# Modulation's weight chunks asked for by GpSimd instead of SyncE, and the gate maxima's rows spread by a store and a load instead of matmuls

## The chip, the core and the metric

One core of one Trainium2 chip runs the whole kernel. The metric is the device time in microseconds of one execution. All engines (TensorE or PE, VectorE or DVE, ScalarE or ACT, GpSimd or POOL, and SyncE or SP, which only issues transfers) work side by side and wait for each other through semaphores. SP, ACT and POOL can each ask for DMA transfers. The transfers that SP and ACT ask for run as "hardware_dynamic" queues in the profile, those of POOL as the "software_dynamic" queue. All share the same 16 DMA engines.

## The reference, cut to what matters

Two networks follow each other on 256 tokens of width 1024, in float32. Two places of them are touched.

```
# first_block: a conditioning vector makes six rows of 1024 per layer and stream
m  = (silu(c)     @ w_mod[i] + b_mod[i]).reshape(bsz, 6, d)     # w_mod: (2, 1024, 6144)
mc = (silu(c_ctx) @ w_mod[i] + b_mod[i]).reshape(6, d)
h_lat   = x * (1.0 + s1) + sh1
mix_lat = chunk_mlp(h_lat, ...)        # gelu(h @ a_w_in), norm, spatial mixing, @ a_w_out
x = layer_norm(DN_ALPHA * x + g1 * mix_lat, ...)
ffn_lat = peer_ffn(x * (1.0 + s2) + sh2, ...)   # queries, top 16 of 16384 experts for each of 8 heads
...
# second_block, mlstm: the running maximum m_t of the gates goes into every score's exponent
m_t     = jnp.maximum(log_inter, jnp.max(log_intra, axis=-1))
d_intra = jnp.exp(log_intra - m_t[..., None])
```

## The kernel before, in words

The first block starts with two works side by side. **Modulation** (`condition`) streams `w_mod` as 48 chunks of 1 MB (128 partitions x 2048 numbers) through a ring of 6 landing places. PE multiplies each chunk with the conditioning columns, and the sums become the rows `m`. Eight chunks make one quarter row set (`q`). The rows are stored to DRAM (`modulation`) and read back where the mixer needs them spread over all partitions. **The mixer** (`first_mix`) streams its own weights as 64 chunks of 256 KB through a ring of 4. ACT rounds a chunk to its high part (`weights_high`), DVE makes the low part (`weights_low`), and PE multiplies with both. Five split chunks can stand ready.

What each engine does next is written out by hand. Each work is a generator that yields slot numbers, `Aside.up_to` runs a work up to a slot, and `run` goes through the slots. So each engine has one fixed order, in which modulation and mixer are interleaved: a modulation chunk about every 3.5 slots, a mixer chunk every 2. SP issues both kinds of load in that order. It stops at the first load whose landing place is not free, and all later loads wait behind it. The stores of `m` and the loads of whole rows (`g_row`, `v_rows`, `n_rows`, `x`, `ws`) stand in the same order.

After the mixer's last queries, DVE picks the first experts (`place`), and POOL begins the gathers: 768 transfers of 1 MB (128 rows of 8 KB each), in a ring of 8, which reuse the memory of the modulation chunks. `wait_rows_free` therefore holds the first gather back until all modulation chunks are used and stored. DVE, ACT and PE work off the gathered rows, and the rest of the first block is placed beside that.

The second block has 404 weight chunks of 512 KB and two layers. In each layer four mLSTM heads need the row of running maxima `rows[0:H, 3, P:]` (4 partitions x 256) on all 128 partitions. PE does this for each head `a` with one matmul against `pick_row`, right behind the head's scores. DVE subtracts it from the mask `past` out of PSUM (`logs`), ACT takes the exponential (`probs_set`), and DVE multiplies it with the scores (`weight`).

Of the kernel before, what the change touches and what calls it, by code (L numbers as in the profile page):

```python
# [25 lines left out]
P = 128  # L26
# [127 lines left out]
def condition(k, sem, buf):  # L154
# [20 lines left out]

    def bias(act):
# [72 lines left out]

    made.pool, made.bias, made.sync, made.stores, made.scalar, made.tensor, made.vector = (  # L250
# [5 lines left out]
def first_mix(k, sem, x, h, buf, given_landed, conditioned):  # L256
# [2052 lines left out]
N_COLS, COLS_HELD = 194, 256  # L2309
# [29 lines left out]
def second_block(k, x, out, ahead):  # L2339
# [5 lines left out]
    with ExitStack() as ctx:  # L2345
        def sem(name):
# [21 lines left out]
        v_ones_set, head_scores, logs_set, probs_set, head_weighed, head_sums, den_set, y_set = [  # L2368
            sem(n) for n in ("v_ones_set", "head_scores", "logs_set", "probs_set", "head_weighed", "head_sums", "den_set", "y_set")]
# [9 lines left out]
        def share(*plans):  # L2379
# [6 lines left out]
            warm=[P, P], bias_rows=[P, BIAS_ROWS, NC], wide_row=[P, D], decay=[P, H, 3 * P], cos=[P, SEQ], sin=[P, SEQ],  # L2386
            wgs_high=(gates_in, F32R), wgs_low=(gates_in, F32R),
            r_weight=[P, 2, 3 * P], inverse_diag=[P, 2, P], inverse_row=[P, SEQ],
            stats=[P, 8, 2, 6], moments=[P, 8, 2], spread=[P, 8], root=[P, 8], inverse=[P, 8],
            x_stats=[P, 2, 2, 6], x_moments=[P, 2, 2], x_spread=[P, 2], x_root=[P, 2], x_inverse=[P, 2],  # L2390
            gate_cols=[P, 16], den=[P, H, 2], den_inverse=[P, H, 2])
# [8 lines left out]
        ((_, weights_low, hT_high, hT_low, warm, bias_rows, wide_row, decay, cos, sin, wgs_high, wgs_low,  # L2400
          r_weight, inverse_diag, inverse_row, stats, moments, spread, root, inverse, x_stats, x_moments, x_spread, x_root,
          x_inverse, gate_cols, den, den_inverse), (_, yrT_low), (_, a1, a2, logs, weight), (_, pw, relu), (_, rg), _) = share(
# [3 lines left out]
        pick_row, past = hold(pick_row=[P, H, P], past=[P, SEQ])  # L2406
# [1426 lines left out]
```

## Time and profile before

| | |
|---|---|
| median of 3 runs | 3600.67 us (3595.59 to 3602.92) |
| the profiled execution, its own time | 3596.3 us |
| its span in the trace | 3594.2 us |
| PE busy | 3219.3 us (90%) |
| DVE busy | 2563.8 us (71%) |
| ACT busy | 1787.8 us (50%) |
| POOL busy | 875.9 us (24%) |
| DMA moved | 1157.76 MB, mean 322 GB/s |

The profiled execution took 2.1 us more than its span, and it lies 4.4 us under the median of the runs. An engine's busy share is a mean over stages that have different limits, so the stretches of the windows view matter more than the table. In that view each row is a stretch of the span with the busy time (and count of instructions) of each engine, then the granted TensorE clock as a share of full speed, the mean busy share of the 16 DMA engines, and the GB/s that they moved.

### The profile page before, as it was taken

To read this page: it belongs to the slowest core of one execution; us is meant where nothing else is said; L and a number is where in the kernel's file an instruction comes from. 1 tells how busy PE (TensorE), PEld (TensorE's weight loads), DVE (VectorE), ACT (ScalarE), POOL (GpSimd) and SP (SyncE) were. 2 spreads that over 40 slices of the span, in tenths; PEclk is the share of its full clock that TensorE was granted. 3 is DMA by queue.
4 is the path that set the end of the run, shared out by engine and by line. 5 is a ranking of instruction groups with operands and counts; after the bars stand their busy time and mean duration, and the time that the engine had idled before them with its cause. 6 is when DMAs were issued, how large, how long until landed. Compare 5 with 4: busy or idle time off the path is not lost. (4 is left out here: it accounts for less than half of the span.)

```text
span 3594.2 us, 38113 instructions
## 1 busy us (share of the span) xinstructions
PE 3219.3 (90%) x12760; PEld 2024.0 (56%) x12760; DVE 2563.8 (71%) x5158; ACT 1787.8 (50%) x3870; POOL 875.9 (24%) x778
## 2 busy tenths in 40 slices
PE   6879898898899989887888777889999999999998
PEld 3444444443354434446433222279878989988897
DVE  2577778878887787756877777578666758766675
ACT  2334554544564565544454444355564645555554
POOL 0024444444443444410444444400000000000000
PEclk8999999999999999999899999999999999999999
DMA  9979999999999999972999999966655656565564
GB/s 407 376 284 424 425 425 414 425 426 414 425 407 425 425 415 427 426 310 94 399 423 427 427 427 427 427 215 183 190 174 183 187 184 187 173 190 185 176 188 140
DMA packets 279755, 1157.76 MB, mean 322 GB/s; under 512 B 31059, under 2 KB 33619, under 8 KB 175110
## 3 DMA queue, kind: packets, MB, share of 16 engines
q0 software_dynamic: 110592, 805.36, 53.4%
q1 hardware_dynamic: 168582, 349.73, 29.2%
q8 instruction: 101, 1.65, 0.2%
q14 instruction: 96, 0.79, 0.1%
q10 hardware_dynamic: 384, 0.23, 0.0%
HBM read 1154.07 MB, written 1.15 MB: 321 GB/s over the span
## 5 line engine op out<-in xcount | busy, mean ns | idle before, releaser
L87 PE MATMUL psum<-rows,diag 128*128 128x512 f32 x3072 | 1473.5, 616 | 275.7 <-ACT diag L2246 273.7
L2202 DVE CUSTOM_DVE_ANT_0 rows<-rows,h 128x1024 f32<-128x1024 f32 x768 | 938.2, 1223 | 454.2 <-DMA rows<-in_p_uv,place 450.9
L2098 POOL DMA_INDIRECT rows<-in_p_uv,place x768 | 872.0, 1135 | 1353.1 <-PE psum L87 1053.5
L87 PEld LDWEIGHTS psum<-rows,diag 128*128 128x128 f32 x3072 | 558.5, 193 | 1091.8 <-ACT diag L2246 591.4
L3019 DVE TENSOR_TENSOR weights_low<-landing,weights_high 128x1024 fp32r<-128x1024 f32 x404 | 490.5, 1221 | 285.3 <-ACT weights_high L2966 282.2
L2966 ACT CAST weights_high<-landing 128x1024 fp32r<-128x1024 f32 x402 | 418.6, 1049 | 471.4 <-PE psum L87 328.6
L2233 ACT ACTIVATE acted<-dots 128x1 f32<-128x1 f32 x768 | 155.1, 202 | 835.3 <-DVE dots L2202 833.4
L87 PE MATMUL psum<-weights_high,hT_high 128*128 128x512 f32 x832 | 352.1, 423 | 14.7 <-DVE h L695 6.5
L2246 ACT ACTIVATE diag<-ident,weight 128x128 f32<-128x128 f32 x768 | 308.5, 402 | 70.4 <-ACT weight L2239 0.4
L87 PE MATMUL psum<-weights_high,hT_low 128*128 128x512 f32 x832 | 325.5, 391 | 0.0
L87 PE MATMUL psum<-weights_low,hT_high 128*128 128x512 f32 x832 | 325.4, 391 | 0.0
L2509 PE MATMUL psum<-hT_high,weights_high 128*128 128x256 f32 x1024 | 291.2, 284 | 1.6 <-DVE hT_low L2996 1.4
L2511 PE MATMUL psum<-hT_high,weights_low 128*128 128x256 f32 x1024 | 289.9, 283 | 0.0
L2510 PE MATMUL psum<-hT_low,weights_high 128*128 128x256 f32 x1024 | 289.9, 283 | 0.0
L2239 ACT ACTIVATE weight<-acted,share 128x1 f32<-128x1 f32 x768 | 226.2, 295 | 27.9
L87 PEld LDWEIGHTS psum<-weights_high,hT_high 128*128 128x128 f32 x832 | 156.8, 189 | 85.5 <-issue 26.8
L2509 PEld LDWEIGHTS psum<-hT_high,weights_high 128*128 128x128 f32 x1024 | 196.8, 192 | 3.4 <-issue 1.7
L2510 PEld LDWEIGHTS psum<-hT_low,weights_high 128*128 128x128 f32 x1024 | 196.8, 192 | 0.1
L2511 PEld LDWEIGHTS psum<-hT_high,weights_low 128*128 128x128 f32 x1024 | 196.6, 192 | 0.0
L87 PEld LDWEIGHTS psum<-weights_low,hT_high 128*128 128x128 f32 x832 | 157.1, 189 | 39.6 <-issue 11.0
L87 PEld LDWEIGHTS psum<-weights_high,hT_low 128*128 128x128 f32 x832 | 156.6, 188 | 34.1
L539 ACT CAST weights_high<-landing 128x512 fp32r<-128x512 f32 x128 | 78.3, 612 | 126.5 <-DMA landing<-in_a_w_in 69.1
(464 smaller groups left out, 3952.0 us busy)
## 6 DMA issues: line engine op xcount, KB each, us to landing
landing<-in_w_in SPq DMA_DIRECT2D x192, 512.0 KB, 3.8
landing<-in_w_ff SPq DMA_DIRECT2D x128, 512.0 KB, 4.0
landing<-in_w_mod SPq DMA_DIRECT2D x48, 1024.0 KB, 8.7
landing<-in_a_w_in SPq DMA_DIRECT2D x64, 256.0 KB
landing<-in_w_br SPq DMA_DIRECT2D x32, 512.0 KB, 3.5
rows<-in_p_uv,place POOLq DMA_INDIRECT x768
lat_landing<-in_b_w_in SPq DMA_DIRECT2D x48, 256.0 KB
landing<-in_a_w_out SPq DMA_DIRECT2D x32, 256.0 KB
```

What stands on the lines that cost most here:

```text
L87: return k.nc.tensor.matmul(out, lhsT, rhs, start=first, stop=last)
L539: S.copy(weights.high[:, n % SPLITS], landing[:, n % LANDING]).then_inc(chunk_high, 1)
L2098: k.nc.gpsimd.indirect_dma_start(rows[:, n % ROW_RING, :], None, k.given["p_uv"], bass.IndirectOffsetOnAxis(place[:, g % 4, c:c + 1], 0))\
L2202: V.tensor_tensor_reduce(u, u, token, 1.0, 0.0, ALU.mult, ALU.add, dots[:, g % 4, c:c + 1]).then_inc(dots_done, 1)
L2233: S.activation(acted[:, slot, c:c + 1], dots[:, slot, c:c + 1], ACT.Gelu_apprx_tanh).then_inc(gelu_done, 1)
L2239: S.activation(weight[:, slot, c:c + 1], acted[:, slot, c:c + 1], ACT.Copy, scale=share[:, slot, c:c + 1])\
L2246: S.activation(diag[:, n % DIAG_RING, :], k.ident[:, :], ACT.Copy, scale=weight[:, slot, c:c + 1])\
L2509: nc.tensor.matmul(to, mine.high, tokens.high, start=first, stop=False, skip_group_check=True)
L2510: nc.tensor.matmul(to, mine.high, tokens.low, start=False, stop=False, skip_group_check=True)
L2511: mm = nc.tensor.matmul(to, mine.low, tokens.high, start=False, stop=last, skip_group_check=True)
L2966: S.copy(weights.high[:, n % SPLITS], landing[:, n % LANDING]).then_inc(chunk_high, 1)
L3019: V.tensor_tensor(weights.low[:, n % SPLITS], landing[:, n % LANDING], weights.high[:, n % SPLITS].bitcast(F32), ALU.subtract).then_inc(ch ...
```

## The change

1. **Modulation's loads move from SP to POOL.** The 48 transfers stand in a new function `loads`, which POOL runs after its two memsets and before its index table and gathers. Each waits only for its own landing place. SP keeps the mixer's loads, the rows and the stores.
2. **Two new waits on SP.** The load of `x` waits until 3 modulation chunks are used, and the mixer's first load until 7 are used.
3. **The maxima's rows are spread by transfers.** ACT stores the four rows (4 KB) to a new DRAM tensor `gate_rows`, waits for the store two slots later, and loads them back to all 128 partitions (512 KB) as `m_rows`. The eight `pick_row` matmuls (4 heads x 2 layers) and the `pick_row` constant are gone. DVE reads `m_rows` in place of PSUM, and does so before it waits for the head's scores.
4. Buffers are laid out anew: `m_rows` is new, `past` moves, `warm` shrinks to one column, and `COLS_HELD` is 208, not 256.

```
+    def loads(pool):
+        for n in range(CHUNKS):
+            q, b = n // DB, n % DB
+            if n >= RING:
+                pool.wait_ge(chunk_used, n + 1 - RING)
+            pool.dma_start(landing[:, n % RING, :],
+                           given["w_mod"][q // 3][b * P:(b + 1) * P, q % 3 * WIDTH:(q % 3 + 1) * WIDTH])\
+                .then_inc(chunk_landed[n % RING], 16)
...
         sp.dma_start(cond[:, :, :], given["cond_cols"]).then_inc(cond_landed, 16)
-        for n in range(CHUNKS):
-            q, b = n // DB, n % DB
-            yield SLOTS[0] if n < RING else SLOTS[n - RING] + 0.5
-            if n >= RING:
-                sp.wait_ge(chunk_used, n + 1 - RING)
-            sp.dma_start(landing[:, n % RING, :],
-                         given["w_mod"][q // 3][b * P:(b + 1) * P, q % 3 * WIDTH:(q % 3 + 1) * WIDTH])\
-              .then_inc(chunk_landed[n % RING], 16)
...
+            if n == 0:
+                conditioned.wait_chunks(sp, 7)
             if n >= LANDING:
...
             conditioned.pool(pool)
             mixed1.pool(pool)
+            conditioned.loads(pool)
             chosen1.pool(pool, lambda engine: None, wait_rows_free)
...
             yield AHEAD + 1
+            conditioned.wait_chunks(sp, 3)
             sp.dma_start(x[:, 0:2, :], given["x"].rearrange("o (t p) d -> p (o t) d", p=P)).then_inc(tokens_landed[0], 16)
...
                 act.wait_ge(m_set, layer + 1)
+                act.dma_start(k.gate_rows[layer], rows[0:H, 3, P:]).then_inc(m_row_stored, 16)
                 S.activation(spare[0:H, :], li[0:H, :], ACT.Exp, scale=-1.0).then_inc(least_set, 1)
+                yield base + 22
+                act.wait_ge(m_row_stored, 16 * (layer + 1))
+                if layer > 0:
+                    act.wait_ge(logs_set, layer * H)
+                act.dma_start(m_rows[:, :, :].rearrange("p a t -> p (a t)"),
+                              k.gate_rows[layer].rearrange("a t -> (a t)").partition_broadcast(P)).then_inc(m_row_landed, 16)
...
-                        causal_scores(bank, qk, a)
-                        matmul(k, k.psum[:, bank + 1, 0:SEQ], pick_row[0:H, a, :], rows[0:H, 3, P:], True, True)\
-                            .then_inc(head_scores, 1)
+                        causal_scores(bank, qk, a).then_inc(head_scores, 1)
...
-                        dve.wait_ge(head_scores, layer * H + a + 1)
-                        V.scalar_tensor_tensor(mine[:, 0:SEQ], k.psum[:, bank + 1, 0:SEQ], -1.0, past[:, :], ALU.mult, ALU.add)
+                        if a == 0:
+                            dve.wait_ge(m_row_landed, 16 * (layer + 1))
+                            dve.wait_ge(more_landed, 64)
+                        if a >= 2:
+                            dve.wait_ge(probs_set, layer * H + a - 1)
+                        V.scalar_tensor_tensor(mine[:, 0:SEQ], m_rows[:, a, 0:SEQ], -1.0, past[:, :], ALU.mult, ALU.add)
...
                         yield base + 2
+                        dve.wait_ge(head_scores, layer * H + a + 1)
```

SP's queue at the very start of the program, before the change. `mod_used` counts modulation chunks that PE has used, `mix_low` mixer chunks that DVE has split:

```order
L186 DMA cond<-in_cond_cols 128x16
L193 DMA landing<-in_w_mod 128x2048 x6
L193 DMA landing<-in_w_mod 128x2048 [waits mod_used]
L3643 DMA x<-in_x 128x2x1024
L193 DMA landing<-in_w_mod 128x2048 [waits mod_used] x4
L321 DMA landing<-in_a_w_in 128x512
L193 DMA landing<-in_w_mod 128x2048 [waits mod_used] x2
L321 DMA landing<-in_a_w_in 128x512
```

The same place on SP, and behind it what POOL now issues:

```order
L196 DMA cond<-in_cond_cols 128x16
L3669 DMA x<-in_x 128x2x1024 [waits mod_used]
L329 DMA landing<-in_a_w_in 128x512 [waits mod_used]
L329 DMA landing<-in_a_w_in 128x512 x3
L204 DMA modulation<-m 2x512 [waits mod_taken]
```

```order
L174 MEMSET m 128x3072
L313 MEMSET keys 128x256
L182 DMA landing<-in_w_mod 128x2048 x6
L182 DMA landing<-in_w_mod 128x2048 [waits mod_used] x42
L2095 ISA
```

All modulation loads are gone from SP's order, and the mixer's first four loads stand together.

PE's queue at the first mLSTM head of the second block, before (`qk` are the head's scores):

```order
L87 MATMUL psum<-qk 128x256 x2
L87 MATMUL psum<-qk 128x128 x2
L87 MATMUL psum<-rows,pick_row 128x256
L87 MATMUL psum<-weights_high,hT_high 128x512
L87 MATMUL psum<-weights_low,hT_high 128x512
```

and now:

```order
L87 MATMUL psum<-weights_low,hT_high 128x512
L87 MATMUL psum<-weights_high,hT_low 128x512
L87 MATMUL psum<-qk 128x256 x2
L87 MATMUL psum<-qk 128x128 x2
L87 MATMUL psum<-weights_high,hT_high 128x512
```

The `pick_row` matmul is gone and the next weight chunk's products follow the scores at once.

ACT's queue where the maxima of a layer are ready, before (the CAST rows round weight chunks, the `spare` row is an exponential of the gates):

```order
L2966 CAST weights_high<-landing 128x1024
L2769 ACT_TABLE_LOAD
L2769 ACTIVATE spare<-li 4x256
L2930 ACTIVATE raw<-raw,cols 128x256 x4
L2966 CAST weights_high<-landing 128x1024 x5
```

and now:

```order
L2981 CAST weights_high<-landing 128x1024
L2775 DMA gate_rows<-rows 4x256
L2776 ACT_TABLE_LOAD
L2776 ACTIVATE spare<-li 4x256
L2945 ACTIVATE raw<-raw,cols 128x256 x4
L2981 CAST weights_high<-landing 128x1024 x2
L2783 DMA m_rows<-gate_rows 128x1024
L2981 CAST weights_high<-landing 128x1024 x3
```

The store stands ahead of the table load, and the load of `m_rows` stands two casts later.

## Rows read from the trace of the kernel before

**Rows 1.** The page, part 1: busy time, share and instructions of PE.
```profile
PE 3219.3 (90%) x12760; PEld 2024.0 (56%) x12760; DVE 2563.8 (71%) x5158; ACT 1787.8 (50%) x3870; POOL 875.9 (24%) x778
```

**Rows 2.** Windows view, stages of the whole span.
```profile
0.00:215.00 215.00, 170.73 (x956) 96.43 (x956) 102.81 (x183) 58.74 (x97) 3.55 (x8) 0.90 0.88 345
...
250.00:1550.00 1300.00, 1159.79 (x3196) 563.75 (x3194) 1010.98 (x2412) 690.02 (x1880) 577.29 (x494) 0.98 1.01 422
1550.00:1700.00 150.00, 124.89 (x480) 86.53 (x480) 91.56 (x150) 71.42 (x132) 7.22 (x10) 0.95 0.49 178
...
2380.00:3594.00 1214.00, 1200.34 (x6800) 1046.38 (x6798) 844.56 (x1163) 650.91 (x854) 0.00 (x0) 1.00 0.58 180
```

**Rows 3.** Windows view, stretches of the first stage.
```profile
50.00:95.00 45.00, 44.53 (x231) 24.88 (x228) 15.90 (x27) 14.78 (x24) 0.00 (x0) 1.00 1.02 419
95.00:110.00 15.00, 13.96 (x71) 6.96 (x71) 10.02 (x14) 7.99 (x13) 0.00 (x0) 1.00 0.97 368
110.00:135.00 25.00, 18.27 (x105) 12.38 (x106) 11.14 (x27) 6.60 (x12) 0.00 (x0) 0.86 1.02 419
135.00:165.00 30.00, 30.00 (x160) 17.29 (x159) 15.80 (x22) 8.56 (x13) 0.00 (x0) 1.00 0.98 371
...
175.00:215.00 40.00, 37.34 (x262) 27.73 (x260) 28.99 (x65) 12.68 (x22) 0.30 (x1) 0.90 0.37 124
```

**Rows 4.** Waits view, 50 to 166 us: total, times, longest.
```profile
ACT weights_high L539 <- DMA landing<-in_a_w_in: 36.9, 15, 4.9
...
ACT weights_high L539 <- DMA landing<-in_a_w_out: 20.7, 7, 5.3
```

**Rows 5.** Waits view of SP's queue, 1 to 215 us.
```profile
SPq L193 <- PE psum L87: 49.2, 20, 8.7
SPq L356 <- DMA modulation<-m: 4.7, 1, 4.7
```

**Rows 6.** Timeline from 0 us: start, duration, engine, what.
```profile
0.74 2.66 POOL L174 MEMSET m<- 128x3072 f32 x1 [0.29 <-POOLq L3827]
...
1.19 12.29 SPq L193 DMA_DIRECT2D landing<-in_w_mod  x7
3.34 0.31 POOL L307 MEMSET keys<- 128x256 f32 x1
```

**Rows 7.** Timeline of POOL: the first gather.
```profile
214.69 1.27 POOL L2098 DMA_INDIRECT rows<-in_p_uv,place  x1 [210.88 <-DVE place L2170]
```

**Rows 8.** Windows view, one microsecond behind it.
```profile
216.00:217.00 1.00, 0.76 (x7) 0.55 (x5) 0.00 (x0) 0.21 (x1) 0.73 (x1) 1.00 0.64 98
```

**Rows 9.** Line 330, two 512 KB rows asked for by SP beside the gathers.
```profile
L330 SPq DMA_DIRECT2D u<-modulation x2: 343/550/758, 221.9 to 222.2; - x2
...
DMA to landing us min/median/max: 8.7/10.4/12.0
```

**Rows 10.** Line 193, modulation loads issued between 30 and 100 us.
```profile
DMA to landing us min/median/max: 6.0/8.5/14.0
```

**Rows 11.** Timeline of ACT, the longest wait for a mixer chunk.
```profile
126.39 0.62 ACT L539 CAST weights_high<-landing 128x512 fp32r<-128x512 f32 x1 [5.32 <-DMA landing<-in_a_w_out]
```

**Rows 12.** All pick_row matmuls (each is recorded as two).
```profile
L87 PE MATMUL psum<-rows,pick_row x16: 374/426/478, 2456.7 to 3128.9; 4*128 4x256 f32 x16
```

**Rows 13.** Timeline of PE: one of the eight, and the next instruction.
```profile
2456.74 0.69 PE L87 MATMUL psum<-rows,pick_row 4*128 4x256 f32 x2
2457.36 0.50 PE L87 MATMUL psum<-weights_high,hT_high 128*128 128x512 f32 x1
```

**Rows 14.** Waits view of PE, 2378 us to the end: the longest entry.
```profile
PE psum L87 <- DVE hT_low L2994: 2.2, 2, 1.1
```

**Rows 15.** Timeline of ACT behind the maxima of layer 0.
```profile
2424.69 0.42 ACT L2769 ACTIVATE spare<-li 4x256 f32<-4x256 f32 x1
...
2430.55 1.05 ACT L2966 CAST weights_high<-landing 128x1024 fp32r<-128x1024 f32 x1 [1.00 <-PE psum L87]
```

**Rows 16.** DMA issues: KB each and us from issue to landing.
```profile
out_x<-x SPq DMA_DIRECT2D x4, 256.0 KB, 2.3
```

More of the change, by code:

```diff
@@ L248, in wait_used, with wait_chunks @@
         engine.wait_ge(chunk_used, CHUNKS)
+    def wait_chunks(engine, n):
+        engine.wait_ge(chunk_used, n)
+    made.loads, made.wait_chunks = loads, wait_chunks
     made.pool, made.bias, made.sync, made.stores, made.scalar, made.tensor, made.vector = (
@@ L2308 @@
 COL = {"norm1": 0, "norm2": 8, "norm3": 16, "m": 24, "r": 32, "b_qk": 48, "taps": 64, "tap_bias": 128, "b_r": 144, "b_ff1": 160, "b_gates": 192}
-N_COLS, COLS_HELD = 194, 256
+N_COLS, COLS_HELD = 194, 208
 IN_AT = 4 * D + 2 * HEADS
@@ L2367, in second_block @@
         convolved, conv_acted, roped, gated = [sem(n) for n in ("convolved", "conv_acted", "roped", "gated")]
-        v_ones_set, head_scores, logs_set, probs_set, head_weighed, head_sums, den_set, y_set = [
-            sem(n) for n in ("v_ones_set", "head_scores", "logs_set", "probs_set", "head_weighed", "head_sums", "den_set", "y_set")]
+        v_ones_set, m_row_stored, m_row_landed, head_scores, logs_set, probs_set, head_weighed, head_sums, den_set, y_set = [
+            sem(n) for n in ("v_ones_set", "m_row_stored", "m_row_landed", "head_scores", "logs_set", "probs_set", "head_weighed", "head_sums", "den_set", "y_set")]
         r_scores, r_weighed, r_sums, r_set = [sem(n) for n in ("r_scores", "r_weighed", "r_sums", "r_set")]
@@ L2399, in second_block @@
         weights_high = ahead.weights_high
-        ((_, weights_low, hT_high, hT_low, warm, bias_rows, wide_row, decay, cos, sin, wgs_high, wgs_low,
-          r_weight, inverse_diag, inverse_row, stats, moments, spread, root, inverse, x_stats, x_moments, x_spread, x_root,
-          x_inverse, gate_cols, den, den_inverse), (_, yrT_low), (_, a1, a2, logs, weight), (_, pw, relu), (_, rg), _) = share(
+        ((_, weights_low, hT_high, hT_low, bias_rows, wide_row, decay, cos, sin, wgs_high, wgs_low,
+          r_weight, inverse_diag, inverse_row, past, stats, moments, spread, root, inverse, x_stats, x_moments, x_spread, x_root,
+          x_inverse, gate_cols, den, den_inverse, warm), (_, yrT_low), (_, a1, a2, logs, weight), (_, pw, relu), (_, rg), _) = share(
             first, *shared, dict(lead=[P, LEAD]))
@@ L2405, in second_block @@
         hold(landing=[P, LANDING, PAIR, NC], cols=[P, DEPTH, COLS_HELD], wg=[P, DEPTH, DB, 2 * H])
-        pick_row, past = hold(pick_row=[P, H, P], past=[P, SEQ])
+        m_rows = hold(m_rows=[P, H, SEQ])
         with split_buffers(k, "f", [P, D_FF // P, SEQ]) as f:
@@ L2456, in _ @@
                 if n == LANDING:
-                    for dst, src in ((pick_row[0:H, :, :], given["pick_row"]), (past[:, :], given["past"]),
+                    for dst, src in ((past[:, :], given["past"]),
                                      (cos[:, :], given["rope_cos"]), (sin[:, :], given["rope_sin"]),
@@ L2571, in pe_heads @@
                         pe.wait_ge(gate_cols_set, layer + 1)
-                        pe.wait_ge(more_landed, 80)
+                        pe.wait_ge(more_landed, 64)
                     if a >= 1:
@@ L3278, in dve_rope @@
                     yield base
-                    dve.wait_ge(more_landed, 80)
+                    dve.wait_ge(more_landed, 64)
                     dve.wait_ge(raw_set, layer * 8 + 4 + i + 1)
@@ L3747, in program @@
         k.modulation = nc.dram_tensor("modulation", (2, DEPTH * 6 * D), F32).ap()
+        k.gate_rows = nc.dram_tensor("gate_rows", (DEPTH, HEADS, SEQ), F32).ap()
         with buffers(k, ident=[P, P], ones=[P, P], gap=[P, 96], x=[P, 4, D]) as (k.ident, k.ones, _, x):
@@ L3777, in constants @@
         "past": np.concatenate([np.where(r[None, :] >= r[:, None], 0.0, MASKED), np.zeros((P, P))], axis=1).astype(f),
-        "pick_row": np.repeat(np.eye(HEADS, dtype=f)[:, :, None], P, axis=2),
         "gla_prefix": (same & (r[:, None] <= r[None, :])).astype(f) / f(GLA_TAU),
```

8 lines of the change are left out of this document (4 added, 4 removed).

## The prediction

> **What bounds the kernel now.** I read the page first. PE is busy for 90% of the span [rows 1], but a mean hides that the stages have different limits, so I cut the span into stages with the windows view [rows 2]. From 250 to 1550 us the DMA engines are at share 1.01 and 422 GB/s: these are the gathers, a fixed number of bytes, and a stage like this only shifts as its start shifts. Between 1550 and 1700 us it is other work that has to end (share 0.49). From 2380 us on PE is busy for 1200.34 of 1214 us, while DMA moves 180 GB/s: here PE's instruction count sets the time. PE's longest entry in the waits of that block is 2.2 us in total [rows 14]. So an instruction taken from PE there is gained in full, and nothing else counts there unless it makes PE wait.
>
> The first stage, to 215 us [rows 2], ends with the first gather, which waits for DVE's picks (`place`) and not for the modulation chunks [rows 7]. What comes before the picks splits in two [rows 3]. From 50 to 165 us two things are near their limit together. DMA moves 419 GB/s in 50 to 95 us with PE busy for 44.53 of 45 us. In 135 to 165 us PE is busy for all 30 us and DMA falls to 371 GB/s. From 175 to 215 us DMA is at share 0.37 and PE at 37.34 of 40 us: queries, scores and picks, which no load holds up. So the end of the stage is the time at which the mixer's loads and products are done, plus a tail that the change leaves alone.
>
> **Part one, modulation's loads on POOL.** Who waits for a load in this stage? ACT waits 36.9 + 20.7 = 57.6 us for mixer chunks between 50 and 166 us, in 22 waits [rows 4]. SP itself stands 49.2 us at modulation loads whose landing place is not free, in 20 waits [rows 5], and the mixer's loads queue behind these. That speaks for the change. But ACT's waiting is not all on the path. With DMA at share 1.02 the bytes are what takes long, and the change moves the same bytes. I therefore cost the stage by what it adds to or takes from bytes before the tail.
>
> *A later start, +3.0 us.* SP's first modulation load is issued at 1.19 us. POOL is free for its first at 3.34 + 0.31 = 3.65 us [rows 6], which is 2.5 us later. The trace has no plain load from POOL. The nearest row is the first gather: issued at 214.69, and in 216 to 217 us the first 98 GB/s [rows 7, 8]. At 422 GB/s that is 0.23 us of moving, so about 2.1 us pass from request to first bytes. SP has a latency too. The lag lies between 2.5 (equal latencies) and 4.6 us (none on SP). I take 3.0, since a latency of near the same size on SP is likely. From 50 to 165 us the DMA engines are hardly ever out of work [rows 3], so all of it counts.
>
> *More unneeded bytes, +2 us.* Before, a modulation chunk lands 8.5 us (median) after its request, since all loads share one queue [rows 10]. The other direction can be read beside the gathers: two rows of 512 KB asked for together land 8.7 us and 12.0 us after their requests at 221.9 and 222.2 us [rows 9]. The second took 3.6 us alone, so 0.524 MB / 3.6 us = 146 GB/s, a third of the total, while 1 MB gathers got the rest. Half a megabyte against one: it looks as if one transfer of each queue is served in turn. A 256 KB mixer chunk against 1 MB modulation chunks would then get a fifth, 85 GB/s, or 3.1 us a chunk, as long as modulation has requests open. Modulation's ring of 6 would fill first and stay fuller. From nothing to all of the ring's missing part, which I estimate from 8.5 us at 2.5 us a chunk (1.049 MB / 422 GB/s) as 8.5 / 2.5 - 1 = 2.4 chunks, this brings forward 0 to 2.4 chunks or 0 to 6 us. I take 2, because once the ring is full modulation asks only as fast as PE uses.
>
> The Trainium skill, DMA: Bandwidth & Descriptors, section Queues, rings and completion order, says that each DMA engine round-robins between the queues it has work for, a packet at a time. The third above agrees with it in this trace.
>
> *Smoother DMA, -2.0 us.* In 95 to 110 us DMA moved 368 GB/s instead of the 422 of the gathers, which is (1 - 368/422) x 15 = 1.9 us of lost moving with PE not full (13.96 of 15). POOL would fill this hole. The dip of 135 to 165 us, (1 - 371/422) x 30 = 3.6 us, lies beside a full PE and gives nothing.
>
> *The stall, -2.0 us.* Between 110 and 135 us PE is idle for 25 - 18.27 = 6.7 us [rows 3]. Of this 5.32 us are ACT's longest wait [rows 11]: SP stands 4.7 us for the stores of `m` [rows 5] and has then three 512 KB rows to ask for before the mixer's next chunk. The wait for the stores stays as it is. What falls away is the modulation chunks ahead of the rows in the queue. Bounds are 0 and 6.7 us; as DMA was at share 1.02 in this stretch, most of it is bytes, so I take 2.0.
>
> Sum of part one: 3.0 + 2.0 - 2.0 - 2.0 = **+1.0 us** at the first gather, and the same at the end, since the gathers behind it run at the DMA limit. The bounds together would be 2.5 + 0 - 1.9 - 6.7 = -6.1 us and 4.6 + 6 - 0 - 0 = +10.6 us. SP's saved issues are worth nothing: its queue waits, and is not short of time [rows 5]. The last gather condition, all modulation chunks used and stored, has the tail's length as its cover.
>
> **Part two, the rows by transfers.** PE loses the 16 records, eight matmuls [rows 12]. Start to next start is 2457.36 - 2456.74 = 0.62 us [rows 13], so 8 x 0.62 = **-5.0 us**. Bounds: 0.5 us each if the switch behind the four-row matmul costs the same behind the scores (-4.0), and 0.69 each (-5.5).
>
> The cost is on ACT. It issues a store and a load for each layer, and its table load now stands behind the store's wait for the maxima. I bound an issue between 0 and 1 us, so some 1 to 3 us later casts in all. ACT has cover: a few casts on it waits for PE to free a split place, 1.00 us long at 2430.55 us [rows 15], and up to four split chunks stand ready, each several microseconds of PE. The wait for the store comes after the exponential, four activations and two casts, from 2424.69 us, which is some 4 us. The only small store in reach, 256 KB of output, lands in 2.3 us [rows 16]. So the wait is covered. If it took twice that, ACT would stand a microsecond more, still inside the ring. The row load of 512 KB has the time to the first head, at 2456.74 us, over 25 us [rows 13]. DVE's two subtractions run as before, only earlier than the scores. DMA has room at share 0.58 [rows 2]. I put 0 on all of this, with +0 to +3 us as bound.
>
> **Sum.** -5.0 + 1.0 = -4.0 us, made against the profiled execution: 3596.3 - 4.0 = 3592.3 us. This execution is 4.4 us under the median of the runs, and the forecast in terms of the median is 3600.67 - 4.0 = **3596.7 us**. A measurement of this kernel tells about 0.2% from no change, 7.2 us, so I forecast no change that can be told.
>
> **The rivals.**
> A. *The mixer gets its own fast lane.* If the DMA engines give SP's queue its fill, mixer chunks no longer stand behind megabytes that are needed later. The whole idle time of PE in 110 to 135 us goes (-6.7), the hole at 95 us (-1.9), and half of the ring's unneeded 6 MB, 3 x 2.5 = 7.5 us, is not yet loaded when the mixer is done; PE's own limit leaves about half of that sum. 3.0 - (6.7 + 1.9 + 7.5)/2 = -5.0, with part two -10.0: **3590.6 us**. For it: the 57.6 us of ACT's waits and the 49.2 us of SP's. Against it: DMA at 1.02, and the third share.
> B. *Slower: the mixer is starved.* At 85 GB/s and 3.1 us a chunk it would be behind PE, which takes a chunk every two slots. While the ring fills, at the start and after each group of rows, PE waits. The price is the upper bound with all its terms, +10.6, and rows at a third share: the three rows of the stall take 3 x 3.6 = 10.8 us where they took 3 x 1.2, so up to +7 more. 10.6 + 7 - 5.0 = +12.6: **3613 us**. It is slower than before as soon as part one costs over 5.0 us, and tellably so over 12.2. Against it: modulation can be six chunks ahead and no more, then it yields.
> C. *Moving the loads does nothing but start later.* +3.0 - 5.0 = -2.0: 3598.7 us. The Trainium skill, DMA: Bandwidth & Descriptors, section Issuing engines are not separate DMA queues, says that issuing on several engines saves only the issuing time; that rule speaks against part one and comes out here. The share of 1.02 agrees.
> D. *The row transfers stall PE* in the second block: over +3 us only if the store takes more than 10 us. I see nothing for it.
>
> **How the numbers follow.** My forecast 0.42, C 0.22 (also within 0.2%), A 0.24, B 0.09, D 0.03. A's 3590.6 lies beyond 7.2 us under the median, and the low edge of my own forecast too: faster 0.28. Slower by over 0.2% needs nearly all of B: 0.08. Same 0.64. For the range I go down to A with a few microseconds for its terms, 3586, and up to the upper bound of part one, 3600.67 + 10.6 - 5.0 = 3606.
>
> **What the changed profile would show.** The first POOL load at 3.7 us and the first gather at 214.7 + 1 us (A: 209 or earlier; B: 222 or later); DMA steadier in 95 to 110 us; ACT's waits for mixer chunks shorter if A, longer if B; from the first weight products of the second block to its end 5 us less, with no PE wait at the heads. I am wrong if the queues share otherwise than in thirds, or if a stage between 1550 and 1750 us swallows or enlarges the shift.

## The result and the profile after

The change made the kernel slower: 3613.8 us median (3610.9 to 3617.5, five runs) against 3600.3 us (3595.6 to 3602.9, five runs). The ratio over all runs is 1.0044, 95% interval 1.0033 to 1.0055, so 12 to 20 us; the two medians alone differ by 13.6 us. The prediction was 3596.7 us with a range of 3586 to 3606. The profiled execution took 3612.0 us, its span was 3610.0, which is 15.8 us more than the span before.

I read the new profile in the order in which the prediction promised signs. First comes GpSimd's timeline, with its first request and the first gather, to be held against [rows 6, 7].

```profile
3.34 0.31 POOL L313 MEMSET keys<- 128x256 f32 x1
3.59 2.84 POOL L182 DMA_DIRECT2D landing<-in_w_mod  x5
...
229.81 1.18 POOL L2106 DMA_INDIRECT rows<-in_p_uv,place  x1 [35.20 <-DVE place L2178]
```

The first request leaves at 3.59 us, as foretold. The first gather is at 229.81 us where it was at 214.69: 15.1 us late. The prediction had written "B: 222 or later" for the starved mixer. Then the windows view, in the cuts of [rows 3]; its columns are PE, PEld, DVE, ACT, POOL busy, PE's granted clock, DMA share and GB/s.

```profile
50.00:95.00 45.00, 33.37 (x150) 17.54 (x148) 10.65 (x17) 11.04 (x17) 4.22 (x8) 0.84 0.94 362
95.00:110.00 15.00, 15.00 (x78) 8.56 (x77) 6.99 (x13) 6.16 (x10) 2.11 (x4) 1.00 1.00 366
110.00:135.00 25.00, 24.73 (x141) 14.15 (x139) 13.77 (x23) 9.45 (x16) 3.16 (x6) 1.00 1.01 406
135.00:165.00 30.00, 21.42 (x112) 13.50 (x109) 11.84 (x23) 8.23 (x14) 2.74 (x6) 0.83 0.78 288
175.00:215.00 40.00, 32.10 (x222) 18.98 (x221) 26.77 (x40) 12.63 (x23) 2.80 (x6) 0.91 0.70 256
```

Between 50 and 95 us PE was busy for 44.53 of 45 us; now it has 33.37. The old stall at 110 to 135 us is indeed gone (24.73 of 25 us), but a new one stands at 135 to 165 us. The bytes that were not moved there come in 175 to 215 us, where DMA had room before: 256 GB/s against 124. Finer windows show how such a stall looks:

```profile
135.00:140.00 5.00, 0.09 (x4) 0.00 (x0) 0.00 (x0) 0.00 (x0) 0.53 (x1) 0.91 1.02 420
140.00:145.00 5.00, 1.33 (x6) 1.36 (x7) 2.17 (x4) 2.23 (x5) 0.00 (x0) 0.50 0.94 374
145.00:150.00 5.00, 5.00 (x22) 3.99 (x24) 3.26 (x10) 0.74 (x2) 0.00 (x0) 0.56 0.36 121
150.00:155.00 5.00, 5.00 (x31) 2.66 (x24) 1.63 (x3) 1.71 (x3) 0.53 (x1) 1.00 0.53 177
```

First PE stands while the DMA engines are full (420 and 374 GB/s); when PE runs again they are two thirds empty (0.36). The idle PE and the idle DMA engines are both a loss. The waits view of 50 to 180 us says who waited for what (total, times, longest):

```profile
POOL landing L182 <- PE psum L87: 115.4, 28, 15.1
DVE weights_low L601 <- ACT weights_high L547: 70.3, 28, 10.4
ACT weights_high L547 <- DMA landing<-in_a_w_in: 54.0, 18, 10.0
...
ACT weights_high L547 <- DMA landing<-in_a_w_out: 25.9, 10, 8.3
```

ACT's waits for mixer chunks went from 57.6 us [rows 4] to 54.0 + 25.9 = 79.9 us, and the longest from 5.3 to 10.0 us. GpSimd, meanwhile, stands 115.4 us with no free place for a chunk: the modulation had all it could hold while the mixer was short. The granted clock also fell, to 0.84 of full speed in 50 to 95 us and to 0.50 in 140 to 145 us, behind 5 us in which PE had been busy for 0.09. In 145 to 150 us PE is busy throughout at 0.56 and has 22 matmul records, in the next 5 us at 1.00 it has 31. So part of the 15.1 us is paid behind the stalls.

The second surprise is in the second block. The prediction had -5.0 us there. In these windows each block is taken from its first gate matmul to the end, before and after:

```profile
2378.86:3594.20 1215.34, 1201.48 (x6810) 1047.46 (x6807) 845.70 (x1164) 651.80 (x854) 0.00 (x0) 1.00 0.58 180
```

```profile
2393.16:3610.00 1216.84, 1203.00 (x6794) 1045.12 (x6791) 845.37 (x1164) 651.66 (x854) 0.00 (x0) 1.00 0.58 181
```

PE has the 16 records fewer, and yet the block is 1.50 us longer and PE 1.52 us busier, at the same granted clock. (Between the first gather and the block the changed kernel is 0.8 us shorter, so 15.1 - 0.8 + 1.5 makes the 15.8 us of the spans.) So some matmuls became longer. The groups of PE's instructions by form, in the second block, name them. Busy time and mean ns of one stand behind the bar; of the three forms of each operand one is shown. Kernel before:

```profile
L87 PE MATMUL psum<-weights_low,hT_high 128*128 128x512 f32 x640 | 249.4, 390 | 0.0
L87 PE MATMUL psum<-weights_low,f_high 128*128 128x512 f32 x256 | 99.6, 389 | 0.0
L87 PE MATMUL psum<-weights_low,yrT_high 128*128 128x512 f32 x128 | 49.8, 389 | 0.0
L87 PE MATMUL psum<-weights_low,ymT_high 128*128 128x512 f32 x64 | 25.0, 391 | 0.0
L87 PE MATMUL psum<-weights_low,pT_high 128*128 128x512 f32 x16 | 6.2, 389 | 0.0
```

Changed kernel:

```profile
L87 PE MATMUL psum<-weights_low,hT_high 128*128 128x512 f32 x640 | 249.4, 390 | 0.0
L87 PE MATMUL psum<-weights_low,f_high 128*128 128x512 f32 x256 | 101.0, 394 | 0.0
L87 PE MATMUL psum<-weights_low,yrT_high 128*128 128x512 f32 x128 | 50.6, 395 | 0.0
L87 PE MATMUL psum<-weights_low,ymT_high 128*128 128x512 f32 x64 | 25.3, 395 | 0.0
L87 PE MATMUL psum<-weights_low,pT_high 128*128 128x512 f32 x16 | 6.3, 395 | 0.0
```

`hT` kept its place in SBUF (the on-chip memory that the engines read) and its 390 ns. The four others (`f`, `yrT`'s high part, `ymT`, `pT`) lie behind `m_rows`, and are loaded as PE's stationary operand (the one that is loaded as weights), 128 columns or 512 bytes a partition at a time. They had moved by 160 columns: `COLS_HELD` took 2 x 48 = 96 away, and `m_rows` (4 x 256) in place of `pick_row` and `past` (4 x 128 + 256) added 256. By the program's addresses they started at multiples of 512 bytes before and start 128 bytes behind one now.

So there are two losses to explain, and each needed its own test: 15 us before the first gather, and some 7 us in the second block that ate the gain of part two.

### The profile page after: what moved, and what is told of

Read it like the earlier page. It is cut to its first block and busy times, and to the rows that moved or that the text cites. A ratio compares the mean times of both kernels' runs of the same rounds, so it can differ in the third digit from the quotient of the medians.

```text
span 3610.0 us, 38095 instructions
## 1 busy us (share of the span) xinstructions
PE 3230.4 (89%) x12744; PEld 2023.3 (56%) x12744; DVE 2563.1 (71%) x5158; ACT 1786.8 (49%) x3870; POOL 895.8 (25%) x826
```

## The experiments

The times are medians, and each ratio is against the kernel before on the same chip (3597.8 to 3598.7 us). Two readings of the profile serve throughout: the **first gather**, which tells the first stage, and the **block**, from its first gate matmul to the end. Each is read from one profiled execution. The block repeats within 0.1 us where its code and layout are the same. The first gather does not: five kernels with one queue and the same first stage have it at 214.7, 215.3, 215.4, 216.3 and 217.0 us, and three with the new queue at 229.8, 232.2 and 234.7. So the queue, with its chunks in one piece and the waits kept, costs 232.2 - 215.7 = 16.5 us there by the means, and a difference of 2 or 3 us in one profile tells nothing.

| kernel | us | ratio (95%) | first gather | block |
|---|---|---|---|---|
| before | 3597.8 to 3600.3 | 1 | 214.69 | 1215.3 |
| changed | 3613.8 | 1.0044 (1.0033 to 1.0055) | 229.81 | 1216.8 |
| e1 rows alone | 3599.7 | 1.0005 (0.9996 to 1.0014) | 217.04 | 1216.8 |
| e2 queue alone | 3611.4 | 1.0039 (1.0025 to 1.0053) | 232.23 | 1215.4 |
| e3 layout alone | 3605.9 | 1.0023 (1.0013 to 1.0033) | 215.36 | 1223.1 |
| e4 rows, aligned | 3590.3 | 0.9981 (0.9972 to 0.9990) | 216.29 | 1209.1 |
| e5 residues | 3604.9 | one run | 215.27 | 1223.2 |
| e6 queue, no waits | 3609.7 | 1.0034 (1.0021 to 1.0046) | 226.56 | 1215.4 |
| e7 queue, split | 3604.3 | 1.0018 (1.0009 to 1.0028) | 221.64 | 1215.4 |
| e8 queue, two ahead | 3628.3 | 1.0087 (1.0070 to 1.0104) | 244.97 | 1215.3 |
| e9 split, no waits | 3604.7 | 1.0016 (1.0007 to 1.0026) | 221.77 | 1215.4 |
| e10 and early | 3608.2 | 1.0028 (1.0016 to 1.0040) | 227.04 | 1215.3 |
| e11 all, early | 3602.7 | 1.0012 (1.0003 to 1.0021) | 227.79 | 1209.2 |
| e12 whole, aligned | 3606.5 | 1.0021 (1.0011 to 1.0030) | 234.69 | 1209.2 |
| e13 early, DVE clears | 3603.5 | 1.0012 (1.0002 to 1.0022) | 221.19 | 1215.3 |
| e14 late start, one queue | 3600.0 | 1.0004 (0.9995 to 1.0014) | 216.21 | 1215.3 |
| e15 all mended | 3595.5 | 0.9993 (0.9983 to 1.0002) | 220.89 | 1209.2 |

### The two parts alone

**e1** takes the changed kernel and gives the modulation's loads back to SyncE, without the two waits.

> The rows by transfers with the layout that comes with them, the modulation's loads back on SyncE's queue and its two new waits gone. Theory (two effects of equal size in the second block: about 3.1 us a layer saved at the heads, about 3.5 to 4 us a layer lost in matmuls whose operands moved by 160 columns in SBUF): 3600 to 3602 us, first gather at about 214.7 us, the 216 matmuls behind the heads at 50.3 us a layer as in the changed kernel. Rival (the slower matmuls of the second block come from the first part, which shifts the block against something): 3594 us and 49.0 us for those matmuls.

3599.7 us, block 1216.8. The 216 matmuls of the expectation are a stretch of the chain that ended last, once in each layer: 49.02 us in the kernel before, 50.35 us in the changed one and 50.35 us here. The slower matmuls are there without the new queue; the rival falls. The time is 0.3 us under the expected range.

**e2** puts part one into the kernel before, and nothing of part two.

> The modulation's loads on GpSimd's queue and SyncE's two new waits, with the gate maxima's rows still picked by matmuls and the layout of before. Theory (the mixer's transfers are starved, one effect, all of it before the first gather): first gather at 229 to 231 us, and 3614 to 3615 us, so more than the whole change costs less the rows' part. Rival (the whole change's loss needs both parts): under 3608 us.

3611.4 us, first gather 232.23 us, block as before. The whole loss of the first stage is the queue's. The time is 2.6 us under what the theory said, the gather 1.2 us over it; it is not the rival's.

### The layout

**e3** is the kernel before with one unused gap:

```
-        pick_row, past = hold(pick_row=[P, H, P], past=[P, SEQ])
+        pick_row, past, _ = hold(pick_row=[P, H, P], past=[P, SEQ], gap=[P, 160])
```

> The kernel before with an unused gap of 160 columns (640 bytes a partition) behind the picking rows and the mask, so that all that lies behind them in the second block stands where the changed kernel has it; not one instruction differs. Theory (the address of a matmul's operands costs 2.5% of it): 3606 to 3608 us, 216 matmuls behind the heads 50.3 us a layer. Rival (the address does nothing; the row transfers or ScalarE's two issues slow them): 3600 us and 49.0 us.

The block, with not one instruction changed, took 1223.12 us for 1215.34:

```profile
2382.78:3605.90 1223.12, 1209.28 (x6810) 1048.27 (x6807) 845.94 (x1164) 651.81 (x854) 0.00 (x0) 1.00 0.58 179
```

That is +7.8 us from addresses alone, and 3605.9 us in time. The size can be counted. `f` has 768 matmuls in the block, `yrT` 384, `ymT` 192, `pT` 48: 1392 in all, so 7.8 us / 1392 = 5.6 ns each in the mean.

The rule "a moved operand is slower" is a little too simple for the rows. `yrT_low` lies ahead of the gap and stands at the same address in both kernels, but its 128 matmuls, which alternate with those of `yrT_high`, lengthened too. First the kernel before, then e3:

```profile
L87 PE MATMUL psum<-weights_high,yrT_low 128*128 128x512 f32 x128 | 49.8, 389 | 0.0
```

```profile
L87 PE MATMUL psum<-weights_high,yrT_low 128*128 128x512 f32 x128 | 50.8, 397 | 0.0
```

On the other side, the score matmuls load `qk` and `rraw` as weights. These are plain float32, moved as far, and kept their times: 379 and 386 ns at 256 columns. So the cost is shown for the matmuls of 512 columns in fp32r (the format in which the high and low parts are held), and for a neighbour of such ones, and not for every load from such an address.

**e4** is e1 with `COLS_HELD` at 256 again, so the shift is 256 columns and not 160:

```
-N_COLS, COLS_HELD = 194, 208
+N_COLS, COLS_HELD = 194, 256
```

> As the rows alone, but the columns' buffer at its old size (256 a layer), so what lies behind moves by 256 columns (1,024 bytes) against the kernel before and not by 160. Theory (address, and what counts is its remainder at some power of two up to 1,024 bytes): 3593.5 to 3595 us, the 216 matmuls at 49.0 us. If what counts is another distance (as between two operands): between 3594 and 3602 us. Rival (the row transfers slow the matmuls): 3600 to 3602 us, as the rows alone.

```profile
2380.10:3589.20 1209.10, 1195.22 (x6794) 1044.23 (x6791) 845.41 (x1164) 651.61 (x854) 0.00 (x0) 1.00 0.58 182
```

The block is 6.2 us shorter than before, all moved operands are back at the times that they had (389 to 391 ns; one form of `ymT` had 403 and has it again), the 216 matmuls take 49.02 us, and the kernel takes 3590.3 us. That is 3 us less than the theory's lowest. This is the version that beats both.

**e5** asks which remainder matters, by giving each operand its own.

> The kernel before with small unused gaps, so that the four operands that the matmuls of the second block load as weights start at different distances behind a multiple of 512 bytes: f at 64, yrT's high part at 128, ymT at 256, pT at 384 (before: all at 0; in the changed kernel: all at 128). No instruction differs. Theory A (a weight load wants each partition's 512 bytes to start at a multiple of 512): all four at 394 to 397 ns a matmul where the kernel before has 389 to 391, and about 3605 us. Theory B (a multiple of 256 is enough): ymT stays at 391 ns, the other three go to 394 to 397. Theory C (only 128 off is bad): f, ymT and pT stay at 390. The hT matmuls keep 390 and 397 ns in each.

```profile
L87 PE MATMUL psum<-weights_low,hT_high 128*128 128x512 f32 x640 | 249.3, 390 | 0.0
L87 PE MATMUL psum<-weights_low,f_high 128*128 128x512 f32 x256 | 101.2, 396 | 0.0
L87 PE MATMUL psum<-weights_low,yrT_high 128*128 128x512 f32 x128 | 50.6, 395 | 0.0
L87 PE MATMUL psum<-weights_low,ymT_high 128*128 128x512 f32 x64 | 24.9, 390 | 0.0
L87 PE MATMUL psum<-weights_low,pT_high 128*128 128x512 f32 x16 | 6.3, 395 | 0.0
```

`ymT`, 256 bytes behind a multiple of 512, is within 1 ns of its old time; `f` at 64, `yrT` at 128 and `pT` at 384 all pay. Theory B holds: of the four starts tried, the one at 256 bytes is free.

**e12** is the changed kernel with `COLS_HELD` at 256.

> The changed kernel with the columns' buffer at its old size of 256 and nothing else. If the layout's loss is the same beside the new queue: 3605 to 3607 us (the changed kernel's 3613.8 less 7 to 8), second block 6 us shorter than in the kernel before. If the slower weight loads came with the new queue: 3613 us.

3606.5 us and a block of 1209.2 us: the layout's loss is the same beside the new queue, and the two are independent.

### The queue

**e6** leaves out SyncE's waits for 3 and 7 used chunks.

> The modulation's loads on GpSimd's queue as before, but without SyncE's two new waits (for 3 and 7 used chunks), the rest as in the kernel before. Theory one (the two queues' shares starve the mixer all the time while both are full): first gather within 4 us of the one with the waits (228 to 233 us), 3608 to 3613 us. Theory two (the waits hold back the mixer's first six chunks, 29.4 us where before had 19.8, and the chain never recovers it): first gather at 217 to 221 us and 3598 to 3602 us.

First gather 226.56 us, between the bands of the two theories, but its time of 3609.7 us is theory one's (e2 has 3611.4), and with split chunks (e7, e9) the waits make no difference. The waits are at most a small part. Leaving them out also has a price of its own: `x` and the mixer's first chunks are then asked for first, and PE's first matmul waits for its modulation chunk until 14.01 us, where it started at 11.21 us in e2.

**e7** keeps every byte and wait, and cuts each modulation chunk in four:

```
-            pool.dma_start(landing[:, n % RING, :], ...
+            for j in range(4):
+                pool.dma_start(landing[:, n % RING, j * NC:(j + 1) * NC], ...
```

> The modulation's chunks on GpSimd's queue, each asked for in four transfers of 256 KB with 2 KB a partition, as the mixer's are, in place of one of 1 MB with 8 KB a partition; the waits are kept. Theory one (each DMA engine takes turns between the queues by descriptor, so a queue with 8 KB pieces gets four times the bytes of one with 2 KB pieces): the mixer gets about half instead of a fifth, its chunks land in 3 to 5 us less, and the first gather comes 6 to 14 us earlier, at 217 to 226 us. Theory two (turns do not depend on the size of a piece; what hurts is that 6 MB are outstanding beside it): first gather within 3 us of the unsplit one, 229 to 235 us.

First gather 221.64 us, 10.6 us earlier than e2, and 3604.3 us. So theory one. More than half of the queue's loss hangs on the size of the other queue's pieces (0.0039 became 0.0018, and 10.6 of the 16.5 us at the first gather). The mixer did not get the half that the theory promised, as the counts under e9 show.

**e8** lets GpSimd have two chunks open in place of six.

> The modulation's chunks on GpSimd's queue with two of them outstanding at a time in place of six (the buffer keeps its six places); the waits are kept. Theory one (the outstanding megabytes starve the mixer): with 2 MB outstanding the mixer's chunks land sooner, the first gather moves from 232 to 218 to 226 us. Theory two (any queue of its own takes its share while at least one transfer is open): landing times stay, and the modulation itself comes later since a transfer's latency is no longer hidden: 230 to 240 us.

It came out at 3628.3 us, but its waits view, 50 to 180 us, is the clearest of all:

```profile
ACT weights_high L547 <- PE psum L87: 75.2, 36, 7.0
...
PE psum L87 <- DMA landing<-in_w_mod: 23.3, 18, 3.3
...
ACT weights_high L547 <- DMA landing<-in_a_w_in: 4.2, 3, 2.2
```

ACT's waits for `a_w_in` fell from 53.9 us in e2 to 4.2. Now PE waits for the modulation itself, and the first gather goes to 244.97 us. Both theories had part of it. Transfers on SP's queue landed sooner with 2 MB open beside them: two `v_rows` of 512 KB in 8.1 and 10.2 us, where e2 has 16.5 and 19.7. And so few open requests do not hide their own latency. The 4.2 us need not be the mixer's gain alone, though: a PE that is held up by the modulation also asks for mixer chunks more slowly. SP's queue moved 2.85 MB in 100 to 130 us, no more than e2's 2.98.

**e9** has both mends, the split and no waits.

> The queue alone with both mends: chunks of the modulation in four transfers of 2 KB a partition, and SyncE's two new waits gone. Theory one (starving by the size of the pieces and the held-back start are two losses that add, 10.6 and 5.7 us of the 17.5): first gather at 214 to 218 us, 3597 to 3600 us. Theory two (they overlap, since both delay the same mixer chunks): 218 to 222 us, 3601 to 3605 us.

First gather 221.77 us: nothing beyond the split. Theory two. The DMA issues of 30 to 100 us (KB each, median us from issue to landing) put the three kernels in a row. One queue (e1):

```profile
landing<-in_a_w_in SPq DMA_DIRECT2D x25, 256.0 KB, 7.5
```

Two queues, modulation in 1 MB with 8 KB a partition (e2):

```profile
landing<-in_a_w_in SPq DMA_DIRECT2D x21, 256.0 KB, 12.6
```

Two queues, modulation in 256 KB with 2 KB a partition (e9):

```profile
landing<-in_a_w_in SPq DMA_DIRECT2D x23, 256.0 KB, 9.2
```

A mixer chunk takes 7.5, 12.6 and 9.2 us. The first gather follows: 217.0, 232.2, 221.8. The middle number is not sharp: e12, with the same queues as e2, has 10.9 us.

The profile also counts what each queue moved: packets, MB, share of the 16 engines. In 110 to 120 us both queues are at work. The `software_dynamic` queue is the modulation's, the `hardware_dynamic` one the mixer's. With chunks in one piece (e2):

```profile
q0 software_dynamic: 416, 3.07, 77.3%
q1 hardware_dynamic: 449, 0.82, 22.7%
```

With split chunks (e9):

```profile
q0 software_dynamic: 878, 2.87, 70.7%
q1 hardware_dynamic: 688, 1.23, 32.3%
```

In e2 the two queues moved nearly the same number of packets, 416 and 449. But the modulation's are 7.4 KB in the mean and the mixer's 1.8 KB, so the mixer got 21% of the bytes. Split, the modulation's packets are 3.3 KB in the mean, and the mixer got 30%. They are smaller but not equal, although each request had 2 KB a partition, and there were still 878 of them to 688. So the mixer did not get its half.

**e10** lets GpSimd ask for the first chunks ahead of its clearing.

> As the last, and GpSimd asks for the first six chunks ahead of its clearing of two buffers, so that the first request leaves near the start (about 0.7 us) and not at 3.6. Theory (the prediction's term for the later start, 3 us): first gather 2 to 4 us before that of the kernel without it. Rival (the start is covered, because the modulation is ahead of the mixer in this layout of queues): within 1 us.

It got slower, 3608.2 us and a first gather of 227.04, which neither expectation had, and it tells nothing of the start. ScalarE's loads of the bias wait for that clearing, which now stood behind 24 issues, and its first activation behind those loads:

```profile
16.95 6.18 ACTq L192 DMA_DIRECT2D m<-in_b_mod  x8
23.16 1.28 ACT L211 ACT_TABLE_LOAD   x1 [23.16 <-issue]
24.45 0.22 ACT L211 ACTIVATE acted<-cond 128x16 f32<-128x16 f32 x1
```

Before, that activation stood at 10.94 us. PE did nothing in the first 24.7 us. **e11**, the whole change with the same early requests, has the same fault. It took 3602.7 us, over the 3595 us up to which the effects would add, and the fault stands in the way of reading it.

> The whole change with everything mended: rows by transfers, the columns' buffer at 256 so that the weights' operands stand on multiples of 512 bytes, the modulation on GpSimd's queue in four transfers a chunk, asked for before the clearing, no new waits on SyncE. If the effects add: the rows aligned alone (3590.3 us) plus what the queue in its mended form still costs (first gather at 213 to 219 us against 214.7 to 217 us): 3588 to 3595 us. If the queue still starves the mixer: over 3595 us.

**e13** moves the clearing to DVE, so the first request can be early without this.

> The queue alone with both mends (first gather 221.8 us), and now GpSimd asks first while VectorE clears the modulation's sums in its place, so that ScalarE, which waits for that clearing, is not held back as in the last such kernel (its first activation came at 24.5 us and not at 10.9). Theory (the later start on GpSimd costs about its delay, 2.4 to 3 us): first gather 218 to 220 us, about 3601.5 us. Rival (what counts is the mixer's share, not when the modulation starts): first gather within 1 us of 221.8, or later.

221.19 us against 221.77: the rival. The first request left at 1.31 us and not at 3.59, and PE's first matmul started at 11.98 us and not at 14.32, and yet the first gather moved by only 0.6 us. **e14** asks the same on one queue: the kernel before, with SyncE's first load of the modulation behind `m_clear`.

> The kernel before with one wait more: SyncE asks for the first chunk of the modulation only when GpSimd has cleared its buffer, at 3.4 us and not at 1.2 to 1.6; one queue as before. Theory (a later start moves the whole first stage by its delay): first gather at 216.7 to 217.5 us, about 3600.5 to 3601 us. Rival (swallowed later in the stage): first gather within 0.5 us of that of the kernel before (214.7 to 215.4).

```profile
3.43 10.05 SPq L194 DMA_DIRECT2D landing<-in_w_mod  x7
13.52 0.44 SPq L3644 DMA_DIRECT2D x<-in_x  x1
```

The first load goes out at 3.43 and not 1.19 us. Yet `x` leaves at 13.52, as it did before. The cover of the later start is PE's first matmul:

```profile
11.21 3.60 PE L87 MATMUL psum<-landing,acted 128*2 128x512 f32 x16 [11.21 <-ACT acted L210]
```

It waits for ScalarE's activation until 11.2 us in both kernels, and SP's seventh load waits for the first chunk used. First gather 216.21 us, between the two expectations and in the middle of the one-queue band; 3600.0 us, with no change inside the interval. A start 2.2 us later costs nothing that can be told.

**e15** is the whole change with every mend.

> The whole change with the operands on multiples of 512 bytes, the modulation in four transfers a chunk, no new waits on SyncE, and VectorE clearing. If the effects add: as the queue with the same mends, less 9 us for the aligned rows: 3592 to 3596 us, so still 2 to 6 us over the rows aligned with one queue (3590.3 us). If the mended queue costs nothing any more: 3589 to 3591 us.

3595.5 us, block 1209.2, first gather 220.89 us: the effects add. It is level with the kernel before and 4 to 5 us over e4. The best second queue I found is still a loss against none; the intervals of e15 and e4 just overlap, but the first gather, at 220.89 us against 214.7 to 217.0, says the same.

## Why the prediction was wrong

**Its forecast was 3596.7 us; the time was 3613.8.** Step by step:

- *A later start, +3.0 us*: about 0. e14 and e13 show it. The prediction assumed that DMA, once busy, never catches up; but PE's first matmul waits for ScalarE's activation until 11.2 us, and SP's seventh load for PE, so at 13.52 us `x` is asked for in both kernels (e14).
- *More unneeded bytes, +2 us of 0 to 6*: **this is the step that failed.** The estimate itself, that a 256 KB chunk against 1 MB chunks gets about a fifth, was right: in 110 to 120 us of e2 the mixer got 21% of the bytes, 0.82 MB in 10 us or 82 GB/s. Its reason was not quite: the queues moved nearly equal numbers of packets there, so the size of the pieces counts and not that of the whole transfer. Chunks landed in 10.9 to 12.6 us and not 7.5, and splitting gave more than half of the loss back. What failed was the price. It counted the bytes that were brought forward and held that a full ring "asks only as fast as PE uses". But PE does its instructions in order. While it stands for a mixer chunk it uses no modulation chunk either, so the delay of a scarce 256 KB is paid in full as idle time, and then the other queue runs dry and the DMA engines idle too (140 to 155 us above). With this term at 0 to 6 the queue part could not pass +10.6; the queue part was 13.6 us in time (e2) and 16.5 us at the first gather.
- *Smoother DMA, -2.0 us*: the sign was wrong. 95 to 110 us stayed at 366 GB/s, and over 50 to 165 us new holes opened. *The stall, -2.0 us*: it did vanish (PE 24.73 of 25 us), only to stand elsewhere. A stall that disappears at its place is not yet a gain.
- *SP's saved issues, nothing*: nothing in the runs speaks against it. SP's new waits were not priced, and e6 and e9 show that they are small.
- *Part two, -5.0 us*: the mechanism was right and the size a little low. The eight matmuls were worth 6.2 us (e4, e12, e15), 0.78 us each, where the prediction had 0.62 and an upper bound of 0.69. It counted from the matmul's start to the next start. What it left out stands ahead of it: the score matmuls start at 2455.34 us and `pick_row` 1.40 us later, while in e4 the same scores start at 2456.74 us and the next matmul 1.23 us later. That is 0.17 us more for each of the eight. PE had no wait at the heads, and the block shows no cost of ACT's issues, as foretold.
- *What was not in the sum*: the layout. **This is the second step that failed.** The change's list said that buffers are laid out anew, and the prediction gave it no term and no reason for giving none. It cost 7.8 us (e3), more than part two gives. The code had a hint: the plan of the first buffers is rounded up to a multiple of P columns, 512 bytes, and one of its gaps has just the 80 columns that round `raw`.

**The rivals.** B named the place and the mechanism of the first stage: gather at 222 or later, PE waiting for starved mixer chunks, even the added waits of ACT. Its 3613 us is near the measured time in part by luck, since it had the second block at -5.0 where it was +1.5. It got 0.09. "Modulation can be six chunks ahead and no more, then it yields" was held against it, and was the wrong argument: six chunks are 6 x 1.049 MB / 422 GB/s = 15 us of all DMA engines, and with two open in place of six ACT hardly waited for the mixer's chunks (e8). C, only a later start, is refuted by e14 and e2. Its rule (the Trainium skill, DMA: Bandwidth & Descriptors, section Issuing engines are not separate DMA queues) says that only issuing time is saved, and none of that shows here. Yet by the landing times and counts above, two issuing engines are two parties to the sharing. The Trainium skill, DMA: Bandwidth & Descriptors, section Queues, rings and completion order, says the same of queues, in turns of packets. The 416 and 449 packets fit that; whether its packet and the profile's are the same thing no run here shows. A, the fast lane, is the opposite of what happened; D did not happen (the block of e4 is 6.2 us shorter).

**Whole sum, from the runs**: queue +14.0 us (0.0039 of 3598, with 9 to 19 in the interval), layout +7.8, rows -6.2: +15.6, with 12 to 20 measured.

**Open.** Two queues still lose 5 to 6 us at the first gather with the chunks split (e7, e9, e15). The packets were then still unequal, 3.3 against 1.8 KB in the mean. No run made them equal, so whether the rest is this, or comes of giving up the one order of need, is not shown. That the queues take turns by packet is the reading that fits 416 to 449. It is not exact: over 100 to 130 us of e2 the counts are 1113 and 1645, and the trace does not say when a queue had nothing open. What SBUF does with a start off 256 bytes is not shown, only what it costs, nor why `yrT_low` pays too.

## What to carry to other kernels

One queue in the order of need is a priority list. Giving a bulk stream its own queue takes that priority away, and here the stream with large pieces and much open won against the one that PE waited for. Before a second queue is added, ask who has more open and in what size, and whether the consumer takes both streams in order.

A change that moves buffers has one more term. Compare the start addresses of what PE loads as weights before and after; here 96 columns saved in one buffer cost more than the edit gained, and giving them back turned the rows' part from no gain (e1) into one of 7.4 us (e4).

Split a change into its parts before judging it: inside this one, slower by 13.6 us, was a part that made the kernel faster once its layout was mended.

## What the runs showed of the hardware

- A matmul of 128x512 f32 words (fp32r) whose stationary operand starts 64, 128 or 384 bytes behind a multiple of 512 takes 394 to 397 ns in the records and not 389 to 391, and costs 5.6 ns more in the mean by the length of the block. At 0 and at 256 bytes it does not (before, e3, e5). One form of `ymT`, at 403 ns before, had 405 at 128 bytes. The matmuls on `yrT_low`, at an unmoved address but between such ones, went from 389 to 397 ns (e3); plain float32 ones on `qk` and `rraw` did not change. The records of the weight loads themselves keep their 188 ns; the matmuls beside them lengthen.
- Two DMA queues with work open shared the DMA engines more nearly by packets than by bytes: 416 packets of 7.4 KB beside 449 of 1.8 KB in 10 us (e2), and 878 of 3.3 KB beside 688 of 1.8 KB (e9). A 256 KB load landed in 7.5 us on one queue (e1), in 10.9 and 12.6 us beside 1 MB loads on the other (e12, e2), and in 9.2 us when these were split (e9).
- PE's granted clock stood at 0.50 of full speed (1.2 GHz) at 140 to 145 us, behind 5 us in which PE had been busy for 0.09 us, and at 0.56 in 145 to 150 us with PE busy throughout. It had 22 matmul records there and 31 in the next 5 us at 1.00.
